# More products with seven multiplications: gates, and r, k and v of the recurrence

## The reference, cut to what matters

```
proj  = h @ w_in
p     = proj[..., OFF_RW:OFF_GATE]           # r, k, v (3 x 2048 columns), and low-rank parts
xs    = p + mu * (prev - p)                  # prev: p of the token before
r, k, v = xs[..., :2048], xs[..., 2048:4096], xs[..., 4096:6144]
...   # per head of 64: a recurrence over the tokens (rwkv7)
gates = sigmoid(proj[..., OFF_GATE:] + b_gate)          # 2 x 2048 columns
mix   = (gates[..., :D] * (o_a @ w_branch_a) + gates[..., D:] * (o_b @ w_branch_b)) @ w_out
```

## Time and profile before

| | |
|---|---|
| median of 3 runs | 3977.06 us (3976.82 to 3977.19) |
| profiled execution, its own time | 3979.2 us |
| its span | 3977.4 us |
| PE busy | 97% |
| DVE, POOL, ACT busy | 44%, 31%, 15% |
| granted TensorE clock, mean | 0.986 |

### The profile page before, as it was taken

The page is one execution under the profiler, slowest core; times in us unless marked ns, Lnnn a source line. Parts: engine busy times, 40 slices in busy tenths (PEclk is TensorE's granted clock), DMA queues, the critical chain, the costliest instruction groups (busy, mean ns, idle before and its releaser), DMA issues.

```text
span 3977.4 us, 65016 instructions
## 1 busy us (share of the span) xinstructions
PE 3846.1 (97%) x28196; PEld 3553.6 (89%) x28196; DVE 1747.7 (44%) x3073; ACT 599.5 (15%) x1314; POOL 1233.2 (31%) x779
## 2 busy tenths in 40 slices
PE   8999999999999998999999999989998899999997
PEld 7888888888878998999999998878797899999997
DVE  1344425550121623111125446552522688888544
ACT  0333311111111111000000000132402211111001
POOL 0000000003320865777760000000250577775000
PEclk9999999999999998999999999999999999999999
DMA  6566654457553443444445454428242344444542
GB/s 229 211 221 219 219 214 159 176 187 225 181 193 139 175 149 117 168 167 168 169 162 170 162 188 183 156 103 227 81 159 85 124 167 168 167 167 159 175 157 78
DMA packets 109117, 668.80 MB, mean 168 GB/s; under 512 B 23056, under 2 KB 27472, under 8 KB 78496
## 3 DMA queue, kind: packets, MB, share of 16 engines
q1 hardware_dynamic: 64208, 549.01, 38.2%
q0 software_dynamic: 21088, 69.73, 6.0%
q10 hardware_dynamic: 23536, 45.92, 3.2%
HBM read 611.34 MB, written 53.25 MB: 167 GB/s over the span
## 4 chain that ended last, share of the span: by engine, by line
PE 92%; DVE 3%; ACT 2%; issue 1%; POOL 1%; POOLq 1%; DVEq 1%; DMA 0%; ACTq 0%
PE product_bank L553 47%; PE product_bank L601 31%; PE product_bank L395 3%; PE mixer_bank L745 1%; PE mixer_bank L761 1%; ACT xT L862 0%; PE mixer_bank L1274 0%; PE mixer_bank L1288 0%; PE mixer_bank L1125 0%; POOL arena L525 0%; POOLq L524 0%; POOL arena L522 0%; POOLq L521 0%; PE product_bank L2237 0%; PE mixer_bank L2199 0%
## 5 line engine op out<-in xcount | busy, mean ns | idle before, releaser
L601 PE MATMUL product_bank<-hT,weight_ring 128*128 128x256 f32 x3712 | 825.0, 380 | 1.6 <-ACT out_stage L640 1.6
L601 PEld LDWEIGHTS product_bank<-hT,weight_ring 128*128 128x128 f32 x3712 | 700.6, 190 | 106.2 <-issue 12.0
L553 PE MATMUL product_bank<-hT,weight_ring 128*128 128x128 f32 x3648 | 453.6, 276 | 11.0 <-DVEq L1631 5.8
L553 PEld LDWEIGHTS product_bank<-hT,weight_ring 128*128 128x128 f32 x3648 | 432.2, 193 | 13.1 <-DVEq L1631 6.0
L553 PE MATMUL product_bank<-arena,weight_ring 128*128 128x128 f32 x3168 | 394.6, 275 | 0.0
L553 PEld LDWEIGHTS product_bank<-arena,weight_ring 128*128 128x128 f32 x3168 | 374.8, 192 | 0.6
L577 DVE TENSOR_TENSOR arena<-product_bank,arena 128x128 f32<-128x128 f32 x126 | 36.7, 291 | 721.1 <-PE product_bank L553 721.1
L520 POOL TENSOR_TENSOR arena<-weight_ring 128x1024 f32<-128x1024 f32 x88 | 211.0, 2398 | 449.7 <-PE product_bank L553 279.6
L2626 DVE SCALAR_TENSOR_TENSOR arena<-arena 128x256 f32<-128x256 f32 x176 | 321.8, 1867 | 14.6 <-ACT arena L2591 11.2
L523 POOL TENSOR_TENSOR weight_ring<-weight_ring 128x1024 f32<-128x1024 f32 x110 | 270.0, 2455 | 0.0
L553 PE MATMUL product_bank<-hT,arena 128*128 128x128 f32 x2016 | 247.4, 277 | 0.1
(11 more groups left out here) (494 smaller groups left out, 5303.5 us busy)
## 6 DMA issues: line engine op xcount, KB each, us to landing
weight_ring<-in_weights SPq DMA_DIRECT2D x213, 2048.0 KB, 8.0
weight_ring<-in_weights SPq DMA_DIRECT2D x128, 512.0 KB, 5.7
weight_ring<-in_weights SPq DMA_DIRECT2D x64, 384.0 KB, 5.7
units<-out_stage ACTq DMA_DIRECT2D x87, 256.0 KB, 7.8
rwkv_keep<-arena ACTq DMA_DIRECT2D x16, 1282.0 KB, 6.3
arena<-rwkv_keep POOLq DMA_DIRECT2D x8, 1280.0 KB, 7.2
arena<-units POOLq DMA_DIRECT2D x36, 256.0 KB, 3.4
arena<-units POOLq DMA_DIRECT2D x48, 128.0 KB, 6.0
```

The source lines that it names most:

```text
L553: mm = pe.matmul(bank[:, at * P:at * P + P], lhs[:, j, :], rhs[:, j, :], start=g == 0 and n in (0, 3) and j == 0, stop=g == n_groups - 1 a ...
L601: mm = pe.matmul(psg[b][:, half * T:half * T + T], lhs, rhs, start=k == 0, stop=k == 15)
```

## The change

Of the 24 units of r, k and v the first of each (3, now `rkv0`) stay ordinary; the other 21 (`rkv7`) and all 16 units of gates become units of seven. Unlike in the other stages, a unit's weights are summed in two groups (g = 0, 1: four of the eight block pairs each), each with its own sum buffer; POOL does it with instructions of 128 x 512. The input sums are made once, in `xT`, which is loaded again from HBM later (with a part of `consts`, whose place serves as temporaries of gates). The result of an `rkv7` unit is not stored: DVE's `recombine_dve` writes it straight to where `shift` reads it (`next_tiles`). Gates are put together in `out_stage`, and ACT stores them. The rw_pack loads move from POOL's queue to ACT's. POOL's queue interleaves the loads of rw2 with the sums of gates, and the loads of the inverted matrices are one DMA per four tiles where they were four; those of rw2's first group move to SP. DVE's order in da and rw2 gets the gates' additions one quarter behind the unit.

```diff
+SEVENS = ("rkv7", "gates", "branch_b", "out", "ffn_in", "ffn_out", "out2", "up2", "down2")
+EARLY = ("rkv7", "gates")
+GROUPS_OF = {n: GROUPS if n in LONG else 2 if n in EARLY else 1 for n in SEVENS}
...
+        def early_quarters(pe, name, src, combined, sums):
+            half = lambda blocks, g: [v[:, 4 * g:4 * g + 4, :] for v in blocks]
+            for u in range(PLAN[name].units):
+                steps = unit_sevens(pe, name, u, lambda g: half(source_blocks(src), g), lambda g: sums(u, g),
+                                    lambda g: half(combined, g))
+                for n, _ in enumerate(steps):
+                    if n in (3, 6, 10):
+                        yield
+                yield
...
         def rw1_pool(pool):
...
-            for b in range(RW_TILES):
-                s = b % 2
-                if b >= 2:
-                    pool.wait_ge(sem("rw1_tile_done"), b - 1)
-                got = sem(f"rw1_in{s}")
-                pool.dma_start(rwp[:, s, :], t_in["rw_pack"][b, :, :]).then_inc(got, 16)
-                for c in range(3):
-                    u = 8 * c + b // 2
-                    unit_stored(pool, "rkv", u)
-                    pool.dma_start(rwx[:, s, c, 1:257], row_of("rkv", u)[:, (b % 2) * T:(b % 2) * T + T])\
-                        .then_inc(got, 16)
...
+            first_tiles(0)
+            first_tiles(1)
+            for u in range(21):
+                for g in range(2):
+                    if u:
+                        group_used(pool, "rkv7", u - 1, g)
+                    sum_weights(pool, "rkv7", u, g, rkv_sums[g])
+                if u == 0:
+                    first_tiles(2)
...
+            def next_tiles(b, c):
+                u = 3 * (b // 2) + c
+                if u < PLAN["rkv7"].units:
+                    recombine_dve(dve, "rkv7", u, rkv_first[u % 2], *rkv_temps, rwx[:, 0, c, 1:257], rwx[:, 1, c, 1:257])
+                    dve.drain()
             def tile(b, s):
+                if s == 1:
+                    next_tiles(b, 1)
...
                 dve.drain().then_inc(sem("rw1_operands"), 1)
                 yield
+                if s == 1:
+                    next_tiles(b, 2)
                 dve.wait_ge(sem("rw1_bonus_sum"), b1)
                 a, z = KEEP_AT["bonus"]
                 dve.tensor_tensor(rw_keep[s][:, a:z], pm[0][:, 256:512], xv, ALU.mult).then_inc(sem("rw1_bonus"), 1)
                 if s == 0:
                     shift(b + 1)
+                    next_tiles(b, 0)
                 dve.wait_ge(sem("rw1_grams"), b1)
...
         def rw2_pool(pool):
...
+            for u, g in [(u, g) for u in range(1, 6) for g in range(2)] + [(6, 0)]:
+                sum_gates(pool, u, g)
+            rw2_operands(pool, 0, 0)
+            between = {(9, 1): (1, 0), (11, 0): (1, 1), (12, 0): (1, None), (13, 1): (2, 0), (15, 0): (2, 1), (15, 1): (2, None)}
...
         def da_pool(pool):
...
+                if h == 7:
+                    sum_gates(pool, 0, 0)
+                    sum_gates(pool, 0, 1)
...
+        def gates_product_dve(dve):
+            yield
+            for u in range(16):
+                for _ in range(4):
+                    yield
+                row, o = gates_kept(u)
+                wait(dve, stored[o], 16 * (row // RING))
+                kept_ = ostage[:, o, :]
+                recombine_dve(dve, "gates", u, gates_first[u % 2], *gates_temps, kept_[:, 0:T], kept_[:, T:2 * T])
+                dve.drain().then_inc(sem("gates_kept"), 1)
```

More of the change, by code:

```diff
@@ L73 @@
              for unit in ORDER]
+ORDER = [("rkv7", 3 * (unit[1] % 8 - 1) + unit[1] // 8) if unit[0] == "rkv" and unit[1] % 8 else
+         ("rkv0", unit[1] // 8) if unit[0] == "rkv" else unit for unit in ORDER]
 LATE = [("ng", 0), ("nv", 0), ("nv", 1), ("mem_k", 1), ("mem_v", 0), ("mem_v", 1)]
@@ L324, in stream_weights @@
                     nsa_loads(sp)
+                if n == UNIT_AT["gates", 6][0]:
+                    store_inverse(sp)
+                if n == UNIT_AT["gates", 8][0]:
+                    rw2_operands(sp, 0, 1)
+                    rw2_rest(sp, 0)
+                if n == UNIT_AT["out", 0][0]:
+                    load_again(sp)
         def run(steps):
@@ new lines, in rw2_rest @@
+        def rw2_rest(eng, n):
+            if n:
+                eng.wait_ge(sem("rw2_group_done"), n)
+            tiles = keep[GT * n:GT * n + GT, :, :].rearrange("g p n -> p g n")
+            eng.dma_start(r2k[:, :, 2 * HALF_W:2 * HALF_W + 2 * T], tiles[:, :, 2 * HALF_W:2 * HALF_W + 2 * T])\
+                .then_inc(sem(rw2_rest_loaded(n)[0]), 16)
+        def rw2_pool(pool):
+            for u, g in [(u, g) for u in range(1, 6) for g in range(2)] + [(6, 0)]:
+                sum_gates(pool, u, g)
+            rw2_operands(pool, 0, 0)
+            between = {(9, 1): (1, 0), (11, 0): (1, 1), (12, 0): (1, None), (13, 1): (2, 0), (15, 0): (2, 1), (15, 1): (2, None)}
+            for u, g in [(6, 1)] + [(u, g) for u in range(7, 16) for g in range(2)]:
+                sum_gates(pool, u, g)
+                if (u, g) in between:
+                    n, half = between[u, g]
+                    if half is None:
+                        rw2_rest(pool, n)
+                    else:
+                        rw2_operands(pool, n, half)
+            rw2_operands(pool, 3, 0)
+            rw2_operands(pool, 3, 1)
+            rw2_rest(pool, 3)
@@ L1229, in rw2_pe, with rw2_rest_loaded @@
+        def rw2_loads(half, n):
+            if half and n == 0:
+                return "rw2_first_in1", 16 * 7
+            return f"rw2_in{half}", 16 * (8 - half) * (n + 1 - half)
+        def rw2_rest_loaded(n):
+            return ("rw2_in_all", 16 * n) if n else ("rw2_first_in_all", 16)
         def rw2_pe(pe):
@@ L2706, in _ @@
             pe.wait_ge(sem("consts_loaded"), 16)
-            for name, u in RKV_GROUPS[0]:
-                run(unit_quarters(pe, name, u, hT))
-            dense = chain(*(unit_quarters(pe, name, u, hT) for group in RKV_GROUPS[1:] + HEAD_GROUPS for name, u in group),
-                          quarters(pe, "gates", hT),
+            run(quarters(pe, "rkv0", hT))
+            dense = chain(early_quarters(pe, "rkv7", hT, early_combined, lambda u, g: rkv_sums[g]),
+                          *(unit_quarters(pe, name, u, hT) for group in HEAD_GROUPS for name, u in group),
+                          early_quarters(pe, "gates", hT, early_combined, gates_sums_of),
                           quarters(pe, "branch_a", oaT, ready="attn_head_done", count=DA_HEADS))
@@ L2779, in _, with heads_and_inverse @@
             pre_norm_dve(dve, "mix_pre", "g_mix_pre", "mix_in")
-            run(rw1_dve(dve))
-            weave(inv_dve(dve), da_dve(dve), inverse_steps)
-            run(rw2_dve(dve))
+            dve.drain()
+            combine_source_dve(dve, "rkv7", source_blocks(hT), early_combined)
+            def heads_and_inverse():
+                inverse = inv_dve(dve)
+                for n, _ in enumerate(da_dve(dve)):
+                    for _ in range(inverse_steps(n)):
+                        next(inverse, None)
+                    yield
+                run(inverse)
+            elsewhere = (None for _ in range(4 * 45))
+            dense = chain(elsewhere, gates_product_dve(dve))
+            beside(dense, rw1_dve(dve), beside_rw1, RW1_LEAD)
+            beside(dense, heads_and_inverse(), beside_da, DA_LEAD)
+            beside(dense, rw2_dve(dve), beside_rw2, RW2_LEAD)
+            run(dense)
             gates_dve(dve)
             out_dve(dve)
+            dve.wait_ge(sem("x_again"), 16)
             post_norm_dve(dve, "mix_post", "x_mixed")
```

176 lines of the change are left out of this document (121 added, 55 removed).

## The result

The changed kernel takes 4088.94 us (median, 4087.05 to 4093.46) where the one before takes 3977.12: ratio 1.0282, 95% interval 1.0264 to 1.0300. The forecast was 4002. The direction was right, the size was not: +112 us instead of +25.

What follows compares the result with a forecast made beforehand. PE was taken to bound all stages concerned. rw1 +38, the start -5 and gates -8 made +25 us on the profiled 3979.2, so 4004 there and a median of 4002 us; range for 8 of 10: 3958 to 4045.

Steps and rivals of the forecast that it cites:

- PE saves 1.3 us a unit: PE work in units of seven: 12.5 us instead of 13.82, 48 us over 37 units if nothing came late.
- POOL's short instructions, 1.2 to 1.3 us: POOL's 128x512 weight-sum instructions: 1.2 to 1.3 us each, a group's sum 5.2 to 5.5, hardly delaying PE itself.
- POOL paces: Rival: short instructions take 1.45 us, a sum 6.2, operands 6 us late in each rw1 tile; 4054 us, 12%.
- the three waits: PE in rw1, per tile pair: operands 1.0 to 3.6 us, bank 5.6 to 6.1, bonus 1.2 net.
- the rule that the forecast had named and left out of its sum: DVE beside POOL: single-input `tensor_scalar` and `copy` take the exclusive lock too; some 0.7 us a tile, 9 over rw1.
- rw1, +38: First pass of the recurrence: three units' savings against the waits give +5.4 us a tile pair, +38 over seven pairs.
- Gates, -8: Attention and rw2: 16 x 1.3 = 20.8 us saved, less late first sum, DVE chains and rw2 costs; bounds -18 and 0.
- Merged loads in rw2 relieve POOL's queue; no PE wait hung on it: Second pass: merged operand loads ease POOL's DMA queue, with no PE wait depending on it; no size given.
- The normalisation: rw2, second pair: DVE's chain slowed by POOL and shorter quarters, 3 to 4 us a group for 2.4 groups.
- The start, -5: Before and in tile 0: one unit saves 1.3 us, and a short copy replacing ACT's store saves 3.7.
- DVE's busy time in rw1 up by half: Sign to look for in rw1: DVE's busy time rises by half.
- The rival in which it pays: Rival: DVE's operations fit beside POOL's short instructions, rw1 breaks even, -23 us remain; 3954 us, 15%.

Runs made afterwards that it cites:

- e16: e9 with rw2's extra quarter unit at the normalisation moved from behind the X step of a group's last chunk instead of added: 3955.3 us (0.9943).
- e18: e16 with gates as ordinary products again, its placement of loads and quarter unit kept: 3978.0 us (1.0002).
- e11: e8 with the copy of four columns at the end of the operands' chain made by ACT instead of DVE: 3974.8 us (0.9993).
- e4: The whole change plus useless PE matmuls in front of rw1's waits for operands, bonus and bank: 4058.9 us (1.0207).
- e2: The whole change with r, k and v as ordinary units again, only gates of seven: 4014.1 us (1.0093).
- e7: The whole change with the eight operand loads of rw2's first group issued by SP instead of POOL: 4062.6 us (1.0210).
- e15: e11 with one rw2 quarter unit moved from behind the X step of a group's last chunk to the second pair's normalisation: 3956.2 us (0.9945).
- e8: The whole change with a second buffer for r's tiles, units put together at each next tile's step, and all rw2 loads on SP: 4003.6 us (1.0061).
- e5: The change for gates only, r, k and v ordinary, with all rw2 operand loads issued by SP: 3984.7 us (1.0020).
- e9: e5 with the first gates' sums behind the loads of head 6 and one quarter unit added at the second pair's normalisation: 3982.9 us (1.0013).
- e13: The kernel before plus six useless DVE products at the end of each tile's operands' chain: 4022.8 us (1.0115).
- e14: The kernel before plus nine useless DVE products at the end of each tile's operands' chain: 4058.0 us (1.0200).

## Why the prediction was wrong

- **PE saves 1.3 us a unit: right.** Groups of eight instructions of a unit of seven start 0.89 us apart in rw1 at full clock, as in ffn_in (1.78 for sixteen), and e16 against e18 is in keeping with it (22.7 us, with the two other terms named there).
- **POOL's short instructions, 1.2 to 1.3 us: right** (1.27). The rival in which POOL paces fell with it; PE never waited for a sum in rw1.
- **The schedule of rw1: the three waits right in kind, their sum nearly in size.** Worked out 9.3 us a pair of tiles, 65 in seven; measured 72.5. That is in part luck, as the errors cancel: the operands were late by 2.5 us a tile (6.0 in tile 0), not 0.5 to 1.8, bank waits 3.7 a pair where 5.6 to 6.1 were expected, the bonus 1.7 instead of 1.2. A good part of the operands' lateness is the rule that the forecast had named and left out of its sum: the single-input copy (L1062) at 1.23 for 0.17, the `tensor_scalar` L1043 at 0.61 for 0.30. The Trainium skill's page (SBUF — State Buffer, "Who interferes with whom") was right here. e11 shows the copy's part as time; that of L1043 was not tried by itself.
- **rw1, +38: the step that failed.** A wait was charged at its own length. Behind most of those of 2.5 us and more PE ran at 1.2 GHz for up to five us: 30 us by e4, 33 by the busy time. The sum also counts one unit of seven twice (seven pairs of three and the one of the start are 22, there are 21), 1.3 us. 38 + 33 + 1.3 and the 7 us by which the waits were larger make 79 to 80 of the 79.1 measured. From tile 1 on, rw1 before has no waits and clock 1.00. But the warning stood in the earlier trace rows: behind the wait of 4.71 us L1095 takes 1.10 us in tile 0, and in tile 1, without a wait,

```profile
143.48 0.60 PE L1095 MATMUL mixer_bank<-arena 96*128 96x256 f32 x2
```

  The kernel before is at 0.95 from 1261 to 1531 us too, where PE waits 7.2 for ACT.
- **Gates, -8: wrong in sign, +37.0 (e2).** "Merged loads in rw2 relieve POOL's queue; no PE wait hung on it" is the sentence that failed: with sums on POOL, PE waits do hang on that queue. 23.3 us for one sum (in e2 23.5), some 26 with the clock behind it (e7); further sums late by 5.8 in rw2; and in da of e2 9.6 for the first. The normalisation, forecast at 3 to 4 us a group for 2.4 groups (7 to 10), cost 10.5 over four (16.2 for 5.7).
- **The start, -5:** -3.8. **Behind rw2, nothing forecast:** 8.2 us less, 4.5 of it a wait of the kernel before for POOL's first sum that is gone.
- **Slips in the working.** The terms of gates (-20.8, 1 and 1, 11.5) make -7, not -8, and a pair in "POOL paces" (13 less 3.9 and 3 for the bank) makes 12 us, not 13. The 0.48 us for an L2626 alone is L962's in the earlier trace rows, an operation of the same form. None of these decides anything.
- **The signs to look for.** DVE's busy time in rw1 up by half: it rose 62% (185.42 to 300.74). Period of a tile: 28.2 foreseen, and (510.90 - 133.65) / 12 = 31.4 measured, between transposes of tiles 0 and 12:

```profile
133.65 1.54 PE L1180 MATMUL mixer_bank<-consts,arena 128*128 128x128 f32 x6 [6.03 <-DVEq L1063]
...
510.90 1.33 PE L1180 MATMUL mixer_bank<-consts,arena 128*128 128x128 f32 x6 [2.53 <-DVEq L1063]
```

- **The range,** 3958 to 4045, had only costs in it that lie on DVE and POOL; neither the clock nor a queue had an end there. The rival in which it pays gave 3954 us for the kernel as it stands, because DVE's operations would fit between POOL's; they do not. That e15 and e16 end near 3955 is a coincidence: they have other loads and another order, e15 ACT's help besides, and e16 has r, k and v as ordinary products.

## What to carry to other kernels

Where PE was busy without a gap, charge each new wait at its length plus a stretch at half clock: here 1.5 to 3 us on top of most waits of 2.5 us and more, and nothing on top of one of 1.5 that stood alone; so shortening a wait a little can be worth twice what it shortens. A row that is slow behind a wait already there, as L1095 in the earlier trace rows, tells the price beforehand. When an engine that issues DMAs is given arithmetic on the critical path, move its loads to another queue first: eight loads cost 26 us. And where POOL works beside DVE, look at the last instructions of DVE's chain: one tiny copy there, moved to ACT, was worth 29 us.

## What was not expected of the hardware

- A copy of 128x4 on DVE took 1.23 us beside POOL's additions, 0.17 alone: what it pays is POOL's instruction, not its own size.
- POOL stood 19.9, 9.0 and 7.5 us between the first two instructions of a sum when it had issued loads just before; with these on SP the gaps were gone (e7, e8).
- Its first addition since the start was followed by 6.7 to 7.9 us of standing where it came late (831.66 in e5, 799.92 in e9, 1279.73 in the kernel before, 1274.55 in e18), in three of the four with no load issued just before; e9 had issued one. In e9 it was laid where PE did not wait for it. In the whole change the first addition, at 92.56 us, was followed by 1.17, and the first after its rest of 395 us by 1.95. The cause was not tried.
- The slow clock is no sure thing behind a middling wait: 2.91 was followed by it eight times of eight in e13, and 2.5 in all twelve tiles of e8. But one wait of 2.83 in e11, three of about 2.6 in e14, and those of 2.51 to 2.53 in tiles 2, 6 and 10 of the whole change (195.38 above) were not. What decides there is open.
